# Carrying the recurrence's states over 64-step super-chunks, with an extra 32x32 score block inside each

## The chip, the cores and the metric

The kernel runs on one core of a Trainium2 chip. A core has a matrix engine (TensorE, "PE" in the profile), a vector engine (VectorE, "DVE"), a scalar engine (ScalarE, "ACT"), a general engine (GpSimd, "POOL") and DMA queues. The metric is the device time of one launch in microseconds (us), the median of several runs.

## What is computed

One encoder layer on 512 positions of width 1024, all in float32: a gated feed-forward block, a mixer, a second feed-forward block, a final norm. The mixer adds attention and a two-directional gated recurrence with 8 heads of key and value width 64. The recurrence is what the change touches. The reference computes it in chunks of 32 positions:

```
def gated_scan_chunked(q, k, v, log_f):         # HGRN_CHUNK = 32
    b = jnp.cumsum(log_f, axis=3)                # within a chunk
    b_mid = b[:, :, :, C // 2 - 1:C // 2, :]
    b_last = b[:, :, :, C - 1:, :]
    scores = einsum('bhntd,bhnsd->bhnts', q * exp(b - b_mid), k * exp(b_mid - b))
    o_intra = einsum('bhnts,bhnse->bhnte', where(lower, scores, 0), v)
    contrib = einsum('bhnsd,bhnse->bhnde', k * exp(b_last - b), v)
    # state_n = exp(b_last_n) * state_{n-1} + contrib_n, one after the other over the chunks
    o_inter = einsum('bhntd,bhnde->bhnte', q * exp(b), states_in)
    return o_intra + o_inter
```

The chunk length is a matter of how the sum is grouped: any grouping gives the same outputs up to rounding. The backward direction is the same on the flipped sequence.

## The kernel before

Large products (feed-forward, projections, gates) run as "units": 8 tiles of 128 rows, each tile three passes (`w_hi`x`h_hi`, `w_hi`x`h_lo`, `w_lo`x`h_hi`, lines 952 to 954) of 128x128 weights against 512 moving columns. Every weight block is loaded by DMA into `raw`, split by ScalarE into `w_hi` (line 358) and by VectorE into `w_lo` (line 621, the line of a helper through which all two-operand VectorE steps go).

The recurrence is done in 8 steps u, one for each pair of heads and direction (u // 2 is the pair, u % 2 the direction; two heads lie on partitions 0 to 63 and 64 to 127). Each engine runs its own program in an order written out by hand, tied by semaphores. The steps are woven into the last 16 projection units, the "gate units". On TensorE one round u is: first half of a gate unit (12 matmuls); `contributions(u)` (line 1159: keys times values spread over the chunks of a 128-tile, into two banks of PSUM); second half of the gate unit; `key_transposes(u+1)` (line 1137); `chunk_scores(u+1)` (line 1148); in two rounds a further whole gate unit; `outputs(u)` (line 1175: masked scores times values; line 1180: carried state times query, one matmul for each chunk and head).

The other engines prepare the operands. VectorE: `cumulate` (the running sum `b_cum`, line 823, and `k_sc`, its distance from the middle of a chunk), `mask_scores` (line 854), `query_key` (keys and end-query scaled), `scan_states` (line 865, the states by one scan over 64 value columns x 16 chunks = 1024 elements), gate units' evacuation, and the norm of finished heads. ScalarE: the exponentials (line 508 for `q_sc`, line 513 for `decay`, then `k_sc`, `k_end`, `b_cum`). GpSimd: the query's product (line 291), `k_end` (lines 285 and 295), `k_in` (line 273) and `v_exp` (line 308: values repeated and masked by the four chunks of a tile, 1024 elements for each head). `state` and its two PSUM banks (4 and 5) exist once: `contributions(u)` waits for scan u-1, the scan for `outputs(u-1)`.

In the trace a float32 matmul leaves two records (and two weight loads), so 8 matmuls of `chunk_scores` are 16 records.

## Time and profile before

| what | us |
|---|---|
| median of 3 runs | 1236.41 (1235.05 to 1237.25) |
| profiled execution: span from first to last instruction | 1232.8 |
| TensorE busy in that span | 1201.1 |
| VectorE busy | 639.7 |
| ScalarE busy | 434.3 |
| GpSimd busy | 120.7 |
| mean granted TensorE clock | 0.981 |

The profile page has the busy times, the chain of work that ended last, and groups of instructions. The timeline gives records in order of time with idle time before them; the view of windows gives, for any stretch, the busy time of each engine and the granted TensorE clock (1.00 is 2.4 GHz, 0.50 is 1.2 GHz). A page's span is from first to last instruction; the median of the runs is 3.6 us more than the profiled span.

### The profile page before, as it was taken

To read this page: it belongs to the slowest core of one execution; us is meant where nothing else is said; L and a number is where in the kernel's file an instruction comes from. 1 tells how busy PE (TensorE), PEld (TensorE's weight loads), DVE (VectorE), ACT (ScalarE), POOL (GpSimd) and SP (SyncE) were. 2 spreads that over 40 slices of the span, in tenths; PEclk is the share of its full clock that TensorE was granted. 3 is DMA by queue.
4 is the path that set the end of the run, shared out by engine and by line. 5 is a ranking of instruction groups with operands and counts; after the bars stand their busy time and mean duration, and the time that the engine had idled before them with its cause. 6 is when DMAs were issued, how large, how long until landed. Compare 5 with 4: busy or idle time off the path is not lost.

```text
span 1232.8 us, 16220 instructions
## 1 busy us (share of the span) xinstructions
PE 1201.1 (97%) x6128; PEld 969.9 (79%) x6128; DVE 639.7 (52%) x764; ACT 434.3 (35%) x597; POOL 120.7 (10%) x86
## 2 busy tenths in 40 slices
PE   6999999999999999999999999999999999999995
PEld 5788888888887777777777778888888888888883
DVE  4755555543334844444777754755555555542223
ACT  5333322232223435455754433443322233322210
POOL 3000000000001300000454410012000000000101
PEclk9999999999999999999989999999999999999997
DMA  5332223333214221112211011432223322232201
GB/s 176 119 102 90 91 91 102 121 101 105 98 68 171 69 85 52 69 52 69 69 35 35 22 49 60 166 114 89 93 95 102 102 102 86 94 137 94 94 23 68
DMA packets 28843, 109.83 MB, mean 89 GB/s; under 512 B 3456, under 2 KB 3584, under 8 KB 28416
## 3 DMA queue, kind: packets, MB, share of 16 engines
q1 hardware_dynamic: 26784, 101.72, 24.8%
q10 hardware_dynamic: 2016, 7.50, 1.7%
q8 instruction: 31, 0.51, 0.2%
q14 instruction: 12, 0.10, 0.0%
HBM read 105.02 MB, written 4.19 MB: 89 GB/s over the span
## 4 chain that ended last, share of the span: by engine, by line
PE 95%; DVE 3%; ACT 1%; ACTq 0%; issue 0%; DVEq 0%
PE ps L952 28%; PE ps L954 28%; PE ps L953 28%; PE ps L1180 2%; PE ps L1031 1%; PE ps L1040 1%; PE ps L1056 1%; PE ps L1159 1%; PE ps L1175 1%; DVE xT L621 1%; PE ps L1148 0%; PE ps L981 0%; DVE state L865 0%; PE ps L1091 0%; PE ps L1097 0%
## 5 line engine op out<-in xcount | busy, mean ns | idle before, releaser
L952 PE MATMUL ps<-h_hi,w_hi 128*128 128x512 f32 x1040 | 419.0, 403 | 13.5 <-DVE w_lo L621 9.7
L953 PE MATMUL ps<-h_lo,w_hi 128*128 128x512 f32 x1040 | 410.2, 394 | 0.0
L954 PE MATMUL ps<-h_hi,w_lo 128*128 128x512 f32 x1040 | 410.0, 394 | 0.0
L621 DVE TENSOR_TENSOR w_lo<-raw,w_hi 128x1024 fp32r<-128x1024 f32 (+1 forms) x178 | 234.9, 1320 | 157.1 <-ACT w_hi L358 156.8
L952 PEld LDWEIGHTS ps<-h_hi,w_hi 128*128 128x128 f32 x1040 | 198.3, 191 | 70.9 <-issue 15.7
L358 ACT ACTIVATE w_hi<-raw 128x1024 fp32r<-128x1024 f32 (+1 forms) x178 | 196.8, 1108 | 128.7 <-PE ps L954 125.8
L954 PEld LDWEIGHTS ps<-h_hi,w_lo 128*128 128x128 f32 x1040 | 198.4, 191 | 42.7
L953 PEld LDWEIGHTS ps<-h_lo,w_hi 128*128 128x128 f32 x1040 | 198.7, 191 | 42.3 <-issue 1.9
L952 PE MATMUL ps<-g_hi,w_hi 128*128 128x512 f32 x352 | 136.9, 389 | 0.0
L953 PE MATMUL ps<-g_lo,w_hi 128*128 128x512 f32 x352 | 136.9, 389 | 0.0
L954 PE MATMUL ps<-g_hi,w_lo 128*128 128x512 f32 x352 | 136.9, 389 | 0.0
L386 ACT ACTIVATE g_hi<-un 128x512 f32 (+1 forms) x44 | 27.8, 632 | 249.6 <-DVE un L621 249.6
L621 DVE TENSOR_TENSOR un<-ps,rs 128x512 f32<-128x512 f32 x44 | 30.4, 691 | 119.6 <-PE ps L954 119.6
L952 PEld LDWEIGHTS ps<-g_hi,w_hi 128*128 128x128 f32 x352 | 66.1, 188 | 13.8
L953 PEld LDWEIGHTS ps<-g_lo,w_hi 128*128 128x128 f32 x352 | 66.1, 188 | 13.7
L954 PEld LDWEIGHTS ps<-g_hi,w_lo 128*128 128x128 f32 x352 | 66.1, 188 | 13.7
L366 ACT ACTIVATE sq<-xT 128x512 f32 (+1 forms) x24 | 15.2, 632 | 150.5 <-DVE xT L624 150.5
L624 DVE SCALAR_TENSOR_TENSOR xT<-ps,xT 128x512 f32 (+1 forms) x24 | 16.6, 692 | 95.6 <-PE ps L954 95.6
L244 POOL COPY sq_sum<-sq 128x512 f32<-128x512 f32 x3 | 1.8, 612 | 600.9 <-ACT sq L366 600.9
L621 DVE TENSOR_TENSOR g_lo<-un,g_hi 128x512 f32 (+1 forms) x44 | 30.5, 693 | 39.2 <-ACT g_hi L386 39.2
L247 POOL TENSOR_TENSOR sq_sum<-sq_sum,sq 128x512 f32<-128x512 f32 x20 | 26.0, 1298 | 207.9 <-ACT sq L366 207.9
L624 DVE SCALAR_TENSOR_TENSOR h_lo<-xT,gain,h_hi (+1 forms) x24 | 23.3, 989 | 32.9 <-ACT h_hi L368 25.4
(199 smaller groups left out, 1121.4 us busy)
## 6 DMA issues: line engine op xcount, KB each, us to landing
raw<-up_dram SPq DMA_DIRECT2D x88, 512.0 KB, 3.3
raw<-down_dram SPq DMA_DIRECT2D x32, 704.0 KB, 4.0
raw<-proj_dram SPq DMA_DIRECT2D x26, 512.0 KB, 3.3
raw<-gates_dram SPq DMA_DIRECT2D x16, 512.0 KB, 3.2
raw<-branch_dram SPq DMA_DIRECT2D x8, 512.0 KB, 3.3
raw<-wout_dram SPq DMA_DIRECT2D x8, 512.0 KB, 3.3
xT<-xT_dram ACTq DMA_DIRECT2D x8, 256.0 KB, 6.9
x_spill_dram<-xT ACTq DMA_DIRECT2D x1, 2048.0 KB, 7.4
```

The lines of the kernel that those rows point to most:

```text
L247: nc.gpsimd.tensor_tensor(sq_sum[:], sq_sum[:], sq[:], ALU.add).then_inc(sum_done, 1)
L358: A(w_hi[:, cst % 4, 0:width], raw[:, cst % 2, 0:width], ACT.Copy).then_inc(hi_done, 1)
L366: A(sq[:], xT[:, n, :], ACT.Square).then_inc(sq_done, 1)
L386: A(g_hi[:, 2 * it + q, :], un[:], ACT.Copy).then_inc(ghi_done, 1)
L621: return V.tensor_tensor(out, a, b, op)
L624: return V.scalar_tensor_tensor(out, a, s, b, op0, op1)
L952: T.matmul(ps[:, bank, :], w_hi[:, slot, cols], moving_hi(j), start=start and j == 0, stop=False)
L953: T.matmul(ps[:, bank, :], w_hi[:, slot, cols], moving_lo(j), start=False, stop=False)
L954: ins = T.matmul(ps[:, bank, :], w_lo[:, slot, cols], moving_hi(j), start=False, stop=stop and j == tiles - 1)
L1031: T.matmul(ps[:, 2 + a, :], qk[rows, 1 + t, P * qt:P * (qt + 1)], qk[rows, 0, :], start=True, stop=True).then_inc(s_done, 1)
L1040: ins = T.transpose(ps[:, 4 + a, P * j:P * (j + 1)], prob[:, a, P * j:P * (j + 1)], ident)
L1180: ins = T.matmul(ps[rows, 7, cc], state[rows, :, n + 1 if d else n - 1], b_cum[u % 3][rows, cc], start=False, stop=d == 1 and n == NCH - 2)
```

## The change

States are carried over super-chunks of 64 positions. The running sum restarts every 64 positions, the scan has 8 states for each value column and not 16, `v_exp` has two masks for each 128-tile, not four, and `contributions` fills one bank. Inside a super-chunk the score block between its two 32-chunks is new: `chunk_scores` computes it by 16 more matmuls (8 super-chunks, 2 heads), each 64 rows by 32 weight columns with 32 moving columns, from `kq_far`, the later chunk's queries and the earlier chunk's keys times a factor `fac`. `fac` is a difference of two middles (VectorE, 16 elements) and an exponential (ScalarE, 16 elements); `kq_far` is written half by VectorE, half by GpSimd (256 elements each). `state` and its bank exist twice.

```
-        v_exp = [at("v_exp0", 88, [P, ST, HD, 4]), at("v_exp1", 80, [P, ST, HD, 4])]
-        state = at("state", 84, [P, HD, NCH])
+        v_exp = [at("v_exp0", 88, [P, ST, HD, 2]), at("v_exp1", 80, [P, ST, HD, 2])]
+        kq_far = at("kq_far", 82, [P, NSUP, 2, CHUNK])
+        state = [at("state0", 84, [P, HD, NSUP]), at("state1", 86, [P, HD, NSUP])]
...
             def query(u):                                  # GpSimd
                 nc.gpsimd.tensor_tensor(q_sc[:], q_sc[:], hq[:, u // 2, :], ALU.mult).then_inc(qs_done, 1)
+                pool.wait_ge(qs_done, u + 1)
+                pool.wait_ge(fac_done, u + 1)
+                late = 1 - u % 2
+                nc.gpsimd.tensor_tensor(kq_far[:, :, late, :], supers(q_sc[:])[:, :, CHUNK * late:CHUNK * (late + 1)],
+                                        fac[:, u % 2, :, late].unsqueeze(2).to_broadcast([P, NSUP, CHUNK]), ALU.mult).then_inc(qfar_done, 1)
...
-            pool.wait_ge(spilled, 16)
-            nc.gpsimd.memset(decay[1], 0.0).then_inc(zero_done, 1)
...
                 A(q_sc[:], k_sc[u % 2][:], ACT.Exp).then_inc(e1_done, 1)     # ScalarE
                 if u >= 2:
                     act.wait_ge(state_done, u - 1)
+                act.wait_ge(fd_done, u + 1)
+                A(fac[:, u % 2, :, :], fac[:, u % 2, :, :], ACT.Exp).then_inc(fac_done, 1)
-                n = slice(first, first + NCH - 1)
+                n = slice(first, first + NSUP - 1)
...
             def query_key(u):                              # VectorE
                 tt(k_sc[par][:], k_sc[par][:], k_in[par][:], ALU.mult).then_inc(ks_done, 1)
+                dve.wait_ge(ks_done, u + 1)
+                dve.wait_ge(fac_done, u + 1)
+                tt(kq_far[:, :, par, :], supers(k_sc[par][:])[:, :, CHUNK * par:CHUNK * (par + 1)],
+                   fac[:, par, :, par].unsqueeze(2).to_broadcast([P, NSUP, CHUNK]), ALU.mult).then_inc(kfar_done, 1)
...
             def scan_states(u):                            # VectorE
-                if u:
-                    dve.wait_ge(o_done, u)
+                if u >= 2:
+                    dve.wait_ge(o_done, u - 1)
-                con, flat = ps[:, 4:6, :].rearrange("p a b -> p (a b)"), state[:].rearrange("p e n -> p (e n)")
+                con, flat = ps[:, 4 + u % 2, :], state[u % 2][:].rearrange("p e n -> p (e n)")
...
             def chunk_scores(u):                           # TensorE
+                pe.wait_ge(kfar_done, u + 1)
+                pe.wait_ge(qfar_done, u + 1)
+                early, late = u % 2, 1 - u % 2
+                for n in range(NSUP):
+                    s0 = SUPER * (n % 2) + CHUNK * early
+                    cols = slice(SUPER * n + CHUNK * late, SUPER * n + CHUNK * (late + 1))
+                    for a, rows in enumerate(head_rows):
+                        ins = T.matmul(ps[s0:s0 + CHUNK, 2 + a, cols], kq_far[rows, n, early, :], kq_far[rows, n, late, :],
+                                       start=True, stop=True)
...
             def contributions(u):                          # TensorE
-                if u:
-                    pe.wait_ge(state_done, u)
+                if u >= 2:
+                    pe.wait_ge(state_done, u - 1)
                 for j in range(ST):
-                    for half in range(2):
-                        for a, rows in enumerate(head_rows):
-                            ins = T.matmul(ps[rows, 4 + half, :].rearrange("p (e n) -> p e n", n=NCH)[:, :, 4 * j:4 * j + 4],
+                    for a, rows in enumerate(head_rows):
+                        ins = T.matmul(ps[rows, 4 + u % 2, :].rearrange("p (e n) -> p e n", n=NSUP)[:, :, 2 * j:2 * j + 2],
...
             def outputs(u):                                # TensorE
-                    carried = [n for n in range(4 * j, 4 * j + 4) if n != (NCH - 1 if d else 0)]
+                    carried = [n for n in range(2 * j, 2 * j + 2) if n != (NSUP - 1 if d else 0)]
```

The order on TensorE in round 0, from the end of the gate unit's second half on. Before (`q_sc` and `k_sc` are the scaled queries and keys, `sc_m` the masked scores, `b_cum` by then the end-query):

```order
L1137 MATMUL ps<-small,k_end 128x128 x4
L1148 MATMUL ps<-q_sc,k_sc_76 128x128 x8
L1175 MATMUL ps<-sc_m_82,v_h 64x128 x2
L1180 MATMUL ps<-b_cum_72,state 64x32 x6
L1175 MATMUL ps<-sc_m_82,v_h 64x128 x2
L1180 MATMUL ps<-b_cum_72,state 64x32 x8
```

And at the same place of the changed kernel, where line 1137 is 1156, 1148 is 1167, 1175 is 1202 and 1180 is 1207:

```order
L1156 MATMUL ps<-small,k_end 128x128 x4
L1167 MATMUL ps<-q_sc,k_sc_76 128x128 x8
L1175 MATMUL ps<-kq_far 32x32 x16
L1202 MATMUL ps<-sc_m_84,v_h 64x128 x2
L1207 MATMUL ps<-b_cum_72,state_82 64x64 x2
L1202 MATMUL ps<-sc_m_84,v_h 64x128 x2
L1207 MATMUL ps<-b_cum_72,state_82 64x64 x4
```

Sixteen matmuls have come in behind the scores, and the carried part has half as many, each of twice the columns. On VectorE the same round, before, from the second half of `cumulate(1)` to the state scan:

```order
L621 TENSOR_TENSOR k_sc_76<-b_cum_73 128x512
L854 COPY_PREDICATED sc_m_82<-consts,ps 128x1024
L621 TENSOR_TENSOR k_sc_76<-k_sc_76,sq_sum 128x512
L621 TENSOR_TENSOR b_cum_73<-b_cum_73,hq 128x512
L865 SCALAR_TENSOR_TENSOR state<-decay_84,ps 128x1024
```

And in the changed kernel:

```order
L630 TENSOR_TENSOR k_sc_76<-b_cum_73 128x512
L630 TENSOR_TENSOR fac<-b_cum_73 128x16
L873 COPY_PREDICATED sc_m_84<-consts,ps 128x1024
L630 TENSOR_TENSOR k_sc_76<-k_sc_76,sq_sum 128x512
L630 TENSOR_TENSOR kq_far<-k_sc_76,fac 128x8x32
L630 TENSOR_TENSOR b_cum_73<-b_cum_73,hq 128x512
L884 SCALAR_TENSOR_TENSOR state_82<-decay_86,ps 128x512
```

Two short steps stand ahead of the scan, and the scan covers half the elements.

## Rows read from the trace of the kernel before

**Rows 1.** The page: busy times, and the chain that ended last by line.
```profile
span 1232.8 us, 16220 instructions
PE 1201.1 (97%) x6128; PEld 969.9 (79%) x6128; DVE 639.7 (52%) x764; ACT 434.3 (35%) x597; POOL 120.7 (10%) x86
...
PE 95%; DVE 3%; ACT 1%; ACTq 0%; issue 0%; DVEq 0%
```

**Rows 2.** Groups by line, 560 to 760 us: xcount | busy us, mean ns | idle before.
```profile
L1180 PE MATMUL ps<-b_cum,state 64*64 64x32 f32 x480 | 32.6, 277 | 0.0
...
L308 POOL TENSOR_TENSOR v_exp<-v_h,gain 128x1024 f32<-128x1024 f32 x8 | 18.1, 2288 | 8.3 <-PE ps L1159 8.3
L1159 PE MATMUL ps<-v_exp,sq 128*64 128x128 f32 x256 | 15.7, 276 | 0.0
...
L823 DVE TENSOR_TENSOR_SCAN b_cum<-consts,forget 128x512 f32<-128x512 f32 x8 | 9.7, 1214 | 1.4 <-ACT forget L498 1.4
...
L865 DVE TENSOR_TENSOR_SCAN state<-xT,ps 128x1024 f32<-128x1024 f32 x4 | 9.1, 2286 | 10.5 <-PE ps L1159 10.4
...
L513 ACT ACTIVATE decay<-b_cum 128x960 f32<-128x960 f32 x4 | 7.8, 1950 | 0.0
```

**Rows 3.** Timeline of TensorE, round 2: start us, length us, record, xcount.
```profile
650.26 1.97 PE L1159 MATMUL ps<-v_exp,sq 128*64 128x128 f32 x32
652.16 0.50 PE L952 MATMUL ps<-h_hi,w_hi 128*128 128x512 f32 x1
...
655.55 1.16 PE L1148 MATMUL ps<-q_sc,k_sc 64*128 64x128 f32 x16
656.64 0.44 PE L1175 MATMUL ps<-sc_m,v_h 128*64 128x128 f32 x4
...
658.16 1.07 PE L1180 MATMUL ps<-b_cum,state 64*64 64x32 f32 x16
659.15 0.44 PE L1175 MATMUL ps<-sc_m,v_h 128*64 128x128 f32 x4
```

**Rows 4.** Timeline of TensorE: the records ahead of which it idled.
```profile
607.03 1.16 PE L1148 MATMUL ps<-q_sc,k_sc 64*128 64x128 f32 x16
610.45 0.47 PE L952 MATMUL ps<-h_hi,w_hi 128*128 128x512 f32 x1 [2.26 <-DVE xT L621]
...
621.69 0.44 PE L1175 MATMUL ps<-sc_m,v_h 128*64 128x128 f32 x4 [0.27 <-DVE state L865]
...
672.35 0.44 PE L1175 MATMUL ps<-sc_m,v_h 128*64 128x128 f32 x4 [1.04 <-DVE state L865]
```

**Rows 5.** Windows: stretch, length, busy (x) of PE PEld DVE ACT POOL, PEclk.
```profile
610.45:614.96 4.51, 4.51 (x13) 3.13 (x13) 4.48 (x5) 1.04 (x2) 1.72 (x2) 0.62 0.76 234
...
627.25:632.34 5.09, 5.09 (x14) 3.77 (x12) 2.05 (x2) 3.81 (x6) 2.49 (x3) 0.54 0.00 0
...
656.64:661.89 5.25, 5.25 (x78) 4.40 (x76) 5.15 (x5) 3.71 (x5) 3.42 (x3) 1.00 0.30 100
661.89:664.86 2.97, 2.97 (x15) 2.17 (x13) 2.90 (x3) 0.25 (x1) 2.46 (x2) 1.00 0.00 0
...
677.91:683.16 5.25, 5.25 (x14) 4.13 (x13) 2.04 (x2) 4.60 (x8) 2.49 (x3) 0.50 0.01 3
```

**Rows 6.** Windows: a gate unit's 24 matmuls at full clock and in part throttled.
```profile
705.13:710.80 5.67, 5.67 (x27) 4.43 (x25) 5.59 (x6) 0.57 (x2) 1.17 (x2) 1.00 0.38 113
751.28:758.46 7.18, 7.18 (x26) 5.79 (x25) 1.23 (x1) 2.03 (x3) 0.00 (x0) 0.76 0.24 75
```

**Rows 7.** A small ScalarE step: groups by line and shape, whole span.
```profile
L460 ACT ACTIVATE lbt<-lbt 128x16 f32<-128x16 f32 x1 | 0.2, 204 | 0.0
```

**Rows 8.** Timeline of VectorE ahead of the scan of round 3.
```profile
666.17 0.68 DVE L621 TENSOR_TENSOR k_sc<-k_sc,k_in 128x512 f32<-128x512 f32 x1
...
667.37 2.52 DVE L621 TENSOR_TENSOR yb<-o_u,yb 128x512 fp32r<-128x512 f32 x1
669.92 2.29 DVE L865 TENSOR_TENSOR_SCAN state<-xT,ps 128x1024 f32<-128x1024 f32 x1
```

More of the change, by code:

```diff
@@ L38 @@
 CHUNK = 32
-NCH = S // CHUNK
+SUPER = 2 * CHUNK
+NSUP = S // SUPER
 EPS = 1e-6
@@ L95, in build @@
         norm_v, norm_y, norm_t = (sb(n, [P, ST]) for n in ("norm_v", "norm_y", "norm_t"))
-        gain = sb("gain", [P, 42])
+        gain = sb("gain", [P, 40])
+        fac = sb("fac", [P, 2, NSUP, 2])
         gq8 = sb("gq8", [P, 1])
@@ L253, in _ @@
                     accumulate(n == 0, n, 8 * r + n)
-            nc.gpsimd.memset(decay[0], 0.0).then_inc(zero_done, 1)
+            for d in range(2):
+                nc.gpsimd.memset(decay[d], 0.0).then_inc(zero_done, 1)
             for masked in sc_m:
@@ L262, in _ @@
                 nc.gpsimd.tensor_tensor(q_cos[:, m % 2, :], qk[:, m, :], c["cos"], ALU.mult).then_inc(cos_done, 1)
-            chunks = lambda t: t.rearrange("p (n c) -> p n c", c=CHUNK)
+            supers = lambda t: t.rearrange("p (n c) -> p n c", c=SUPER)
             def key(u):
@@ L282, in to_end @@
                     pool.wait_ge(kt_done, u)
-                b3 = chunks(b_cum[u % 3][:])
-                end = b3[:, :, 0 if u % 2 else CHUNK - 1]
-                nc.gpsimd.tensor_tensor(chunks(k_end[:]), end.unsqueeze(2).to_broadcast([P, NCH, CHUNK]), b3,
+                b3 = supers(b_cum[u % 3][:])
+                end = b3[:, :, 0 if u % 2 else SUPER - 1]
+                nc.gpsimd.tensor_tensor(supers(k_end[:]), end.unsqueeze(2).to_broadcast([P, NSUP, SUPER]), b3,
                                         ALU.subtract).then_inc(d3_done, 1)
@@ L304, in values @@
                     pool.wait_ge(pv_done, ITEMS)
-                shape = [P, ST, HD, 4]
+                shape = [P, ST, HD, 2]
                 for a in range(2):
@@ L308, in values @@
                     nc.gpsimd.tensor_tensor(v_exp[a][:], v_h[:, :, HD * h:HD * (h + 1)].unsqueeze(3).to_broadcast(shape),
-                                            gain[:, 38:42].unsqueeze(1).unsqueeze(1).to_broadcast(shape),
+                                            gain[:, 38:40].unsqueeze(1).unsqueeze(1).to_broadcast(shape),
                                             ALU.mult).then_inc(vexp_done, 1)
-            pool.wait_ge(spilled, 16)
-            nc.gpsimd.memset(decay[1], 0.0).then_inc(zero_done, 1)
             key(0)
@@ L506, in exponentials @@
                     act.wait_ge(sc_done, u)
-                b, first, end = b_cum[u % 3], (1, 0)[u % 2], (CHUNK - 1, 0)[u % 2]
+                b, first, end = b_cum[u % 3], (1, 0)[u % 2], (SUPER - 1, 0)[u % 2]
                 A(q_sc[:], k_sc[u % 2][:], ACT.Exp).then_inc(e1_done, 1)
@@ L826, in cumulate @@
                 mid = b3[:, :, CHUNK // 2 if u % 2 else CHUNK // 2 - 1]
-                tt(chunks(k_sc[u % 2][:]), b3, mid.unsqueeze(2).to_broadcast([P, NCH, CHUNK]), ALU.subtract).then_inc(d1_done, 1)
+                tt(chunks(k_sc[u % 2][:]), b3, mid.unsqueeze(2).to_broadcast([P, 2 * NSUP, CHUNK]), ALU.subtract).then_inc(d1_done, 1)
+                b6 = supers(b[:])
+                if u % 2:
+                    tt(fac[:, 1, :, :], b6[:, :, 16:33:16], b6[:, :, 32:49:16], ALU.subtract).then_inc(fd_done, 1)
+                else:
+                    tt(fac[:, 0, :, :], b6[:, :, 31:48:16], b6[:, :, 15:32:16], ALU.subtract).then_inc(fd_done, 1)
             def normalize(t):
@@ L1147, in chunk_scores @@
                     for a, rows in enumerate(head_rows):
-                        ins = T.matmul(ps[:, 2 + a, cols], k_sc[u % 2][rows, cols], q_sc[rows, cols], start=True, stop=True)
+                        T.matmul(ps[:, 2 + a, cols], k_sc[u % 2][rows, cols], q_sc[rows, cols], start=True, stop=True)
+                pe.wait_ge(kfar_done, u + 1)
[7 more added lines that the diff above has]
+                                       start=True, stop=True)
                 ins.then_inc(sc_done, 1)
@@ L1175, in outputs @@
                         T.matmul(ps[rows, 7, cols], v_h[:, j, HD * h:HD * (h + 1)], sc_m[d][:, a, cols], start=d == 0 and j == 0, stop=False)
-                    carried = [n for n in range(4 * j, 4 * j + 4) if n != (NCH - 1 if d else 0)]
+                    carried = [n for n in range(2 * j, 2 * j + 2) if n != (NSUP - 1 if d else 0)]
                     for n in carried:
-                        cc = slice(CHUNK * n, CHUNK * (n + 1))
+                        cc = slice(SUPER * n, SUPER * (n + 1))
                         for rows in head_rows:
-                            ins = T.matmul(ps[rows, 7, cc], state[rows, :, n + 1 if d else n - 1], b_cum[u % 3][rows, cc],
-                                           start=False, stop=d == 1 and n == NCH - 2)
+                            ins = T.matmul(ps[rows, 7, cc], state[d][rows, :, n + 1 if d else n - 1], b_cum[u % 3][rows, cc],
+                                           start=False, stop=d == 1 and n == NSUP - 2)
                 ins.then_inc(o_done, 1)
@@ L1296 @@
     sin = np.sin(ang).astype(np.float32)[:, p % 32].T * np.where(p % HD < 32, -1.0, 1.0)[:, None]
-    keep = np.broadcast_to(pos[None] % CHUNK != 0, (P, S))
-    same = p[:, None] // CHUNK == p[None] // CHUNK
+    keep = np.broadcast_to(pos[None] % SUPER != 0, (P, S))
+    same = p[:, None] // SUPER == p[None] // SUPER
     mask = np.concatenate([same & (p[:, None] <= p[None]), same & (p[:, None] >= p[None])], axis=1)
```

17 lines of the change are left out of this document (9 added, 8 removed).

## The prediction

> **What bounds the kernel now.** I read the page first. TensorE is busy for 97% of the 1232.8 us span and makes 95% of the chain that ended last [rows 1]. So only what TensorE streams, how fast it is clocked and where it idles can move the time; a faster ScalarE or GpSimd is worth nothing by itself. The groups by line over the recurrence's stretch then give what each kind of small matmul costs in sum [rows 2]; the timeline of one undisturbed round gives the spacing [rows 3]; the idle times ahead of TensorE's records are three, 2.26, 0.27 and 1.04 us, together 3.57 us [rows 4]; and the windows show a fourth quantity, time at the lower clock [rows 5, 6].
>
> **The spacing of small matmuls.** One number carries the sum. In round 2 a run of 16 records of line 1180 (32 moving columns) starts at 658.16 and the next work at 659.15: 62 ns for each record [rows 3]. The 32 records of line 1159, with 128 moving columns each, go from 650.26 to 652.16: 59 ns each. The 16 of line 1148, with 128 weight columns and 128 moving ones, go from 655.55 to 656.64: 68 ns each [rows 3]. So four times the columns costs no more: nothing in these rows lies below 59 ns, and a record of 32 or 64 columns costs some 62.5 ns, whatever is in it. Each matmul is two records.
>
> **What goes on TensorE.** Line 1180 has 480 records, 30 matmuls in each of 8 rounds, as 15 of 16 chunks carry a state. With super-chunks it is 7 of 8, 14 matmuls in a round, 224 records. Their 64 moving columns lie between the 32 and the 128 of rows that both stay near 60 ns, so I take 62.5 again; 256 records fewer are 16.0 us less (the upper price of 68 ns would make it 14.8). Line 1159 has 256 records for 15.7 us [rows 2]; half of them go with the same shape (64 value columns x 2 masks is the 128 that 32 x 4 was): 128 x 59 ns = 7.6 us less.
>
> **What comes.** 16 matmuls in each of 8 rounds are 256 records of 64 rows x 32 weight columns with 32 moving columns. The trace has no such tile. The nearest row is line 1180 with the same 32 moving columns: 62.5 ns, 16.0 us in all. From below: if a smaller tile were quicker, nothing shows by how much; 40 ns, an estimate at two thirds of that row, would give 10.2 us, so a gain of 5.8 more. From above: `outputs(2)` takes 5.25 us [rows 5], of which 60 records of line 1180 are 3.75, so each of its four groups of 4 records of line 1175 takes 0.37, or 92 ns a record with the changes of shape around it; at that price the extra block would be 23.6 us, 7.6 more. I take 62.5 as nearest in shape. A change of tile shape costs too: 4 records of line 1175 at 59 ns would be 0.24 us, they take 0.37, so 0.13 us for a switch. The extra block puts one more switch into each round, 8 x 0.13 = 1.0 us. The work on TensorE then changes by -16.0 - 7.6 + 16.0 + 1.0 = -6.6 us. The Trainium skill (TensorEngine Tiling, "Key Properties") says that changing the tiling mode drains the engine, which speaks against the new block; the trace agrees with a price, 0.13 us as just worked out. It also says (TensorE: Matmul & The Clock Gate, "Wait — 56ns, not 53.3ns?") that small matmuls have a floor of about 25 ns, or about 62 ns where the sequencer decodes them; this trace sits at the latter with 62 ns [rows 3], and by the former the extra block would be an estimated 6.4 us.
>
> **Idle time.** The first idle time, 2.26 us, lies right behind `chunk_scores(0)`, whose records started at 607.03 and ran 1.16 us: TensorE waits until 610.45 for a VectorE evacuation [rows 4]. The 32 new records of that round, 2.0 us, fall into this hole, and GpSimd's `v_exp`, two of 2.29 us each before, is halved [rows 2], so VectorE, which runs slowed beside it, isn't later. The hole closes: 2.26 us back. The other two are waits for the state scan. In round 3 VectorE comes to it late, behind `yb` (2.52 us), and the scan takes 2.29 us [rows 8]. A scan of 512 elements is in the trace at 1.21 us (line 823, [rows 2]), 1.1 us less. Against it stand the new steps on VectorE: 16 elements for `fac`, taken at the 0.2 us that ScalarE needs for as many [rows 7], and 256 elements for its half of `kq_far`, which lie between that and the 0.68 us of 512 elements [rows 8], say 0.4. From one scan's start to the next's end that is -1.1 - 1.1 + 0.2 + 0.4 = -1.6 us, while TensorE gets to its place about 1 us later after the extra block than it would relative to the same scan. Both waits (0.27 and 1.04) go. Idle time: -3.6 us.
>
> **The new waits.** `chunk_scores` now waits also for both halves of `kq_far`. ScalarE's new exponential is 0.20 us [rows 7], but `decay` shrinks from 960 to 448 elements, from 1.95 us to an estimated 0.9 at most, worked out in proportion [rows 2], so everything behind it on ScalarE (`k_sc`, `k_end`, `b_cum`) is about 0.8 us earlier, and VectorE's and GpSimd's products with it. Their additions of 0.4 and some 0.8 us are covered by that and by several microseconds that both have in hand: the keys of step 4 are done at 666.9 [rows 8], and TensorE comes for them at some 670.2, the 16 records of `chunk_scores` ahead of the idle time that ended at 672.35 [rows 4]. Cost 0; were the cover gone in a round, that round would lose at most the 0.8 us. What is queued behind that wait on TensorE is `outputs`, and behind it the next gate unit. Double-buffering frees the scan of `outputs(u-1)`, which no idle time of the trace is due to: 0. The cleared `decay` on GpSimd moves ahead of the recurrence, into its long wait: 0.
>
> **The clock.** The granted clock falls to the lower level six times in this stretch. The first time is behind the idle hole: 610.45 to 614.96 at 0.62, 4.51 us for 12 matmuls that take 2.97 at 1.00 [rows 5]: 1.5 us lost. Four more come at the end of `outputs`, with TensorE busy throughout: 627.25 to 632.34 (5.09, so 2.1 lost) and 677.91 to 683.16 (5.25, so 2.3) are two [rows 5]; a second like the first of these and one of 1.3 us are the others. In three rounds the tail of `outputs` also took 5.56 us, not 5.25, 0.3 more each. The sixth is the unit behind round 7, 7.18 us for the 24 matmuls that otherwise take 5.67 [rows 6]: 1.5 us. Summed: 1.5 + 2.1 + 2.1 + 2.3 + 1.3 + 0.9 + 1.5 = 11.7 us. What ran before five of the six is the same: 5.25 us of `outputs`, 3.8 us of it line 1180, which streams 32 columns in a record's 62 ns. Rounds 2, 4 and 5 had the same and didn't fall ([rows 5], 1.00), so it is near the edge. Lines 1148 and 1159, packed with 128 columns, never precede a fall. In the new kernel `outputs` lasts 4 x 0.37 + 28 x 0.0625 = 3.2 us and its carried records stream twice the columns; only the new block, 2.0 us, is as thin as line 1180 was. I judge that most falls go; I leave one, 2.3 us, so -9.4 us.
>
> **The sum.** -6.6 - 3.6 - 9.4 = -19.6 us, a span of 1213.2, and with the 3.6 us by which the median stands above the profiled span, 1217. Nothing behind the recurrence takes it back: there too TensorE's own lines make the chain [rows 1].
>
> **Rivals.** (a) *The clock goes on falling.* New block and `outputs` stand together, 5.3 us of small tiles against 5.25, and a 64x32 tile fills less of the array than line 1180's 64x64 did. If what keeps the clock up is how much of the array works, and not how many columns stream, the five falls with a busy TensorE stay and only the one behind the hole goes: -6.6 - 3.6 - 1.5 = -11.7, 1225. For it: five falls came with no idle time to explain them. Against it: denser `outputs`. (b) *The extra block is dearer or its waits bite*, at 92 ns a record or with 0.8 us of waiting in each round: 7 us on top of either case, 1224 to 1232. (c) *Slower.* The records of the new tile don't overlap: two heads write one partition range, and each record runs for its own length, 271 ns by line 1180's mean of 277 [rows 2], instead of being followed at 62.5. That is 256 x 0.21 = 54 us, some 1270. It decides from where the spacing passes 0.0625 + 19.6/256 = 0.14 us, with case (a)'s clock from 0.11. Against it: lines 1148 and 1180 alternate the same two row groups and do overlap. (d) *It changes nothing*: the new records cancel the carried ones one for one, 256 against 256, and if the clock falls as often and the block costs 92 ns, 1232 to 1236 is left.
>
> **How the numbers follow.** Forecast, falls mostly gone, 1213 to 1221: 0.52. (a), 1221 to 1229: 0.26. (b) beyond these, up to 1233: 0.10. (c): 0.07. (d): 0.05. A measurement of this kernel can tell about 0.2%, 2.5 us, from no change. Faster by more than that is 0.88, within it 0.05, slower 0.07. The range that holds it 8 times in 10 goes from 1211, all falls gone and a slightly cheaper block, to 1229, the upper end of (a).
>
> **What would show it.** Right: line 1180's successor with 224 records at 62 ns spacing, line 1159's with 128 in half the time; the new block at 2.0 us for 32 records; no idle time behind `chunk_scores(0)` nor ahead of `outputs(0)` and `outputs(3)`; gate halves behind `outputs` at 2.97 us and PEclk 1.00, but for one. Wrong: a spacing in the new block well over 68 ns, waits of TensorE for either half of `kq_far`, or 5 us gate halves at 0.5 behind `outputs`.

## The result and the profile after

The changed kernel takes 1207.74 us (median of 4 runs, 1207.26 to 1207.87), against 1235.73 for the kernel before (4 runs, 1233.88 to 1237.25): a ratio of 0.9781, interval 0.9763 to 0.9799, some 28 us faster. I had forecast 1217 with a range of 1211 to 1229. The direction was right; the time lies below the range.

The page of the changed kernel, the lines that answer to [rows 1]:

```profile
span 1205.5 us, 16026 instructions
PE 1173.3 (97%) x6000; PEld 944.8 (78%) x6000; DVE 636.4 (53%) x780; ACT 428.8 (36%) x605; POOL 119.0 (10%) x94
...
PE 95%; DVE 2%; issue 1%; ACT 0%; ACTq 0%; POOL 0%; DVEq 0%; POOLq 0%
```

The span is 27.3 us shorter. All of it lies between the first `key_transposes` and the last `mean_square`. The view of windows over this stretch (length, busy time of PE, PEld, DVE, ACT and POOL, granted clock), up to where each kernel starts its last `mean_square`, first before (line 1128 starts at 758.46):

```profile
606.50:758.46 151.96, 148.39 (x1295) 118.54 (x1294) 101.98 (x88) 59.90 (x81) 52.08 (x34) 0.90 0.14 46
```

and after, with `outputs(1)` and a gate half behind `outputs(0)`:

```profile
606.91:731.51 124.60, 120.54 (x1167) 92.90 (x1166) 98.49 (x102) 55.22 (x88) 50.93 (x41) 1.00 0.16 54
632.34:636.08 3.74, 3.74 (x54) 2.78 (x45) 3.71 (x4) 1.64 (x3) 2.69 (x2) 1.00 0.46 140
623.51:626.45 2.94, 2.94 (x14) 2.18 (x12) 2.42 (x3) 2.57 (x6) 2.46 (x3) 1.00 0.01 4
```

The stretch went from 151.96 to 124.60 us, 27.4 less, and its clock from 0.90 to 1.00: not one fall is left. `outputs` takes 3.74 us where it took 5.25 [rows 5]. The timeline of TensorE in rounds 1 and 2 (start, length, record, xcount) answers to [rows 3]:

```profile
630.86 1.16 PE L1167 MATMUL ps<-q_sc,k_sc 64*128 64x128 f32 x16
631.95 0.46 PE L1175 MATMUL ps<-kq_far 64*32 64x32 f32 x32
632.34 0.44 PE L1202 MATMUL ps<-sc_m,v_h 128*64 128x128 f32 x4
632.71 0.69 PE L1207 MATMUL ps<-b_cum,state 64*64 64x64 f32 x8
633.33 0.44 PE L1202 MATMUL ps<-sc_m,v_h 128*64 128x128 f32 x4
...
635.69 0.46 PE L1207 MATMUL ps<-b_cum,state 64*64 64x64 f32 x4
636.08 0.50 PE L971 MATMUL ps<-h_hi,w_hi 128*128 128x512 f32 x1
...
639.88 1.09 PE L1186 MATMUL ps<-v_exp,sq 128*64 128x128 f32 x16
640.91 0.50 PE L971 MATMUL ps<-h_hi,w_hi 128*128 128x512 f32 x1
```

The 32 records of the new block, which I had priced at 2.0 us, fill 631.95 to 632.34: 0.39 us. The 16 of `contributions` fill 1.03, not 1.90. Eight carried records with the change of shape ahead of them fill 0.62. The idle times, which answer to [rows 4], are others than before:

```profile
609.63 0.47 PE L971 MATMUL ps<-h_hi,w_hi 128*128 128x512 f32 x1 [0.64 <-DVE xT L630]
617.66 0.66 PE L1156 MATMUL ps<-small,k_end 128*128 128x128 f32 x4 [1.10 <-POOL k_end L304]
659.30 0.44 PE L1202 MATMUL ps<-sc_m,v_h 128*64 128x128 f32 x4 [0.89 <-DVE state L884]
...
667.49 1.13 PE L1147 MATMUL ps<-o_ms,consts 128*128 128x512 f32 x2 [1.43 <-ACT o_ms L555]
```

They sum to 4.06 us, and before to 3.57. From these rows the sum, beside the one forecast (the row on the clock is the time that the kernel before lost in its six falls, as the prediction summed it; none is left):

| term | forecast | measured |
|---|---|---|
| carried matmuls (480 to 224 records) | -16.0 | 8 x (3.74 - 5.25) = -12.1 |
| `contributions` | -7.6 | 8 x (1.03 - 1.90) = -7.0 |
| the extra block, with its change of shape | +17.0 | 8 x 0.39 = +3.1 |
| idle time | -3.6 | 4.06 - 3.57 = +0.5 |
| the lower clock | -9.4 | -11.7 |
| sum | -19.6 | -27.2 |

The error is in one term above all, the block: 13.9 us too dear. The carried matmuls (3.9 us less gained than forecast) and the idle time (4.1 us) err the other way. That the measured median lies only 9.3 us under the forecast is luck of this kind: with the block alone set right, the forecast would have been 1203.

### The profile page after: what moved, and what is told of

It is laid out like the page before. It is cut to its first block, busy times and chain, and to the rows that moved or that the text cites. A ratio compares the mean times of both kernels' runs of the same rounds, so it can differ in the third digit from the quotient of the medians.

```text
span 1205.5 us, 16026 instructions
## 1 busy us (share of the span) xinstructions
PE 1173.3 (97%) x6000; PEld 944.8 (78%) x6000; DVE 636.4 (53%) x780; ACT 428.8 (36%) x605; POOL 119.0 (10%) x94
## 4 chain that ended last, share of the span: by engine, by line
PE 95%; DVE 2%; issue 1%; ACT 0%; ACTq 0%; POOL 0%; DVEq 0%; POOLq 0%
PE ps L971 29%; PE ps L973 28%; PE ps L972 28%; PE ps L1050 1%; PE ps L1075 1%; PE ps L1059 1%; PE ps L1207 1%; PE ps L1202 1%; PE ps L1186 1%; PE ps L1167 0%; PE ps L1000 0%; DVE xT L630 0%; PE ps L1110 0%; PE ps L1116 0%; PE ps L1147 0%
## 5 line engine op out<-in xcount | busy, mean ns | idle before, releaser
L971 PE MATMUL ps<-h_hi,w_hi 128*128 128x512 f32 x1040 | 414.5, 399 | 11.9 <-DVE w_lo L630 9.7
L973 PEld LDWEIGHTS ps<-h_hi,w_lo 128*128 128x128 f32 x1040 | 195.9, 188 | 41.4
L972 PEld LDWEIGHTS ps<-h_lo,w_hi 128*128 128x128 f32 x1040 | 196.1, 189 | 41.0 <-issue 1.9
```

The costliest lines, as they stand in the source:

```text
L971: T.matmul(ps[:, bank, :], w_hi[:, slot, cols], moving_hi(j), start=start and j == 0, stop=False)
L972: T.matmul(ps[:, bank, :], w_hi[:, slot, cols], moving_lo(j), start=False, stop=False)
L973: ins = T.matmul(ps[:, bank, :], w_lo[:, slot, cols], moving_hi(j), start=False, stop=stop and j == tiles - 1)
```

## The experiments

Each is an edit of the changed kernel unless it says otherwise. Times of one run stand without an interval. The theory to be tested was the one the prediction rested on, that any small record costs about 60 ns whatever is in it. The changed kernel's own block refuted it at once; what then sets a spacing had three candidates: (A) the weight load, and with it the stride at which the weights lie, (B) adding into sums that a PSUM bank already holds, (C) how many tiles of the array take turns.

**Without the block.** The matmuls of the extra block are left out, and the mask lets only the 32-step blocks through (not shown in the cut):

```
                 for j in range(ST):
                     for a, rows in enumerate(head_rows):
-                        T.matmul(ps[:, 2 + a, cols], ...)
-                for n in range(NSUP):
-                    ...
-                        ins = T.matmul(ps[s0:s0 + CHUNK, 2 + a, cols], kq_far[rows, n, early, :], kq_far[rows, n, late, :], ...)
+                        ins = T.matmul(ps[:, 2 + a, cols], ...)
```

> The changed kernel without the 256 extra records of the score block on TensorE (kq_far is still computed; the 32x32 blocks between the chunks of a super-chunk are left out, and the mask lets only 32-chunks through). The trace of the changed kernel has the block's 32 records in 0.4 us a round. If that is their whole price: 8 x 0.4 = 3.3 us faster than the changed kernel, some 1204.5. If the block costs what I predicted (16 us + 1 us for the change of tile shape) it would be 1191. If the waits for kq_far cost besides, nothing of that goes, since they stay with the last matmul of the scores only as a semaphore on VectorE's and GpSimd's side; the idle ahead of outputs(3) of 0.9 us should then grow to 1.3.

Measured: 1205.32 us (4 runs, 1205.14 to 1205.68; ratio to before 0.9759, 0.9742 to 0.9775), 2.4 us under the changed kernel, and not 17. Idle time ahead of `outputs(3)` rose from 0.89 to 1.52 us and idle time in all from 4.06 to 5.43, so 1.4 of the 3.1 us came back as waiting; the spans differ by 2.2, 0.5 more than that leaves. The block's price is a few microseconds.

**The block twice.**

```
-                for n in range(NSUP):
+                for n in list(range(NSUP)) * 2:
```

> The changed kernel with every matmul of the extra block issued twice (same outputs). At 12.5 ns a record, as its trace shows: +3.2 us, 1211. At 62.5 ns, the spacing of line 1180: +16 us. If the thin block is what brings the clock down, falls of 2 us a piece appear with it; by the theory of too thin a stretch a doubling to 0.8 us is still short and none appears.

Measured: 1208.65 us (one run), 0.9 more. On TensorE the doubled block of round 1, from the timeline:

```profile
632.18 0.76 PE L1175 MATMUL ps<-kq_far 64*32 64x32 f32 x64
632.86 0.44 PE L1202 MATMUL ps<-sc_m,v_h 128*64 128x128 f32 x4
```

64 records in 0.68 us where 32 took 0.39: a further record costs 9 ns. Eight times 0.29 us is 2.3 us of work, of which idle time gave back 0.8 (3.27 us in place of 4.06). No fall of the clock came with it. The measured whole was even less than the expected 3.2, and the spacing of line 1180 was off by a factor of seven for this tile.

**Carried weights packed**, in the changed kernel and in the kernel before. The weights are 64 adjacent words of the same state tile; both kernels so edited leave out the order in which the states lie, so their outputs are not those of the layer:

```
-                            ins = T.matmul(ps[rows, 7, cc], state[d][rows, :, n + 1 if d else n - 1], b_cum[u % 3][rows, cc],
+                            ins = T.matmul(ps[rows, 7, cc], state[d][:].rearrange('p e n -> p (e n)')[rows, HD * (n + 1 if d else n - 1):HD * ((n + 1 if d else n - 1) + 1)], b_cum[u % 3][rows, cc],
```

> The changed kernel, with the weights of the carried matmuls read as 64 adjacent words of the state tile instead of 64 words 32 bytes apart (they are then the wrong states: the order of the states in the outputs is left out; shapes, counts and accumulation stay). Theory A (the stride of the weights sets the spacing): the 28 records of a round go from 78 ns to 60 or less, 8 x 28 x 0.02 = 4 us or more faster, and their weight loads from 213 ns to the 137 ns of the other 64-column loads. Theory B (adding into a PSUM bank that holds sums sets it): 78 ns stay, same time. Theory C (64 weight columns instead of 32, or two tiles in turn instead of four): 78 ns stay too.

> The kernel before with the same edit (weights of line 1180 adjacent, not 64 bytes apart; the order of the states is left out). Theory A: 480 records at 62.5 ns become 480 at some 20 to 40 ns: 11 to 20 us faster, plus the clock falls that go with the shorter stretch. Theories B and C: 62.5 ns stays and the time is that of before.

Measured: 1204.39 us for the changed kernel so edited (4 runs, 1204.09 to 1204.96; ratio 0.9752, 0.9735 to 0.9768) and 1221.65 (one run) for the kernel before so edited, 13.5 us under its neighbours of 1235.14. The timeline of the latter in round 2, at a clock of 1.00:

```profile
650.87 0.54 PE L1180 MATMUL ps<-b_cum,state 64*64 64x32 f32 x12
651.34 0.44 PE L1175 MATMUL ps<-sc_m,v_h 128*64 128x128 f32 x4
651.71 0.66 PE L1180 MATMUL ps<-b_cum,state 64*64 64x32 f32 x16
652.30 0.44 PE L1175 MATMUL ps<-sc_m,v_h 128*64 128x128 f32 x4
```

and of the kernel before as it is, the run of twelve in the same round (the run of sixteen is in [rows 3]):

```profile
657.01 0.85 PE L1180 MATMUL ps<-b_cum,state 64*64 64x32 f32 x12
657.79 0.44 PE L1175 MATMUL ps<-sc_m,v_h 128*64 128x128 f32 x4
```

The changed kernel with packed weights, in round 0:

```profile
619.98 0.33 PE L1207 MATMUL ps<-b_cum,state 64*64 64x64 f32 x4
620.24 0.44 PE L1202 MATMUL ps<-sc_m,v_h 128*64 128x128 f32 x4
620.61 0.45 PE L1207 MATMUL ps<-b_cum,state 64*64 64x64 f32 x8
620.99 0.44 PE L1202 MATMUL ps<-sc_m,v_h 128*64 128x128 f32 x4
```

And the weight loads of the changed kernel, by line, as it is and packed:

```profile
L1207 PEld LDWEIGHTS ps<-b_cum,state 64*64 64x64 f32 x224 | 16.0, 208 | 5.5 <-issue 5.5
```

```profile
L1207 PEld LDWEIGHTS ps<-b_cum,state 64*64 64x64 f32 x224 | 9.0, 133 | 5.5 <-issue 5.5
```

In the kernel before with packed weights twelve records take 0.47 us and sixteen 0.59, so one more costs 29 ns; as it is, twelve take 0.78 and sixteen 0.99, one more 53 ns. In the changed kernel four records take 0.39 us and eight 0.62, one more 58 ns; packed, four take 0.27 and eight 0.38, 28 ns. Shapes, counts and accumulation were left alone. So A holds and B falls: the stride of the weights doubles the spacing, and 32 or 64 moving columns make almost no difference to it. Theory C isn't touched by this, hence the next two. In the changed kernel the time fell by 3.3 us; of the 7 us less work, 2.8 came back as idle time, which rose to 6.89. In the kernel before, `outputs` went from 5.25 to 3.71 us, 12.3 us less in eight rounds, and idle time rose from 3.57 to 9.03; the rest of its 13.5 us, an estimated 6 to 7, is time at the lower clock that is gone (see below).

**The block on two tiles.**

```
-                for n in range(NSUP):
+                for n in (0, 2, 4, 6, 1, 3, 5, 7):
```

> The changed kernel with the block's matmuls in the order of super-chunks 0 2 4 6 1 3 5 7 (same outputs): now two tiles of the array take turns (one column group, two row groups), where four did. If the number of tiles in turn sets the 12.5 ns, the block's spacing doubles to 20 to 25 ns and a round's block takes 0.7 us, 2 to 3 us in all; if the width of the weights does (32 columns and packed), it stays at 0.4 us and the time at 1207.7.

Measured: 1209.0 us (one run), and by the timeline 32 records from 632.29 to 632.82, 0.53 us in place of 0.39. The spacing went from 12 to 17 ns over the whole block: less than double, but the number of tiles in turn does count. C holds in part. The edit changes nothing but the order; what one more record costs with two tiles wasn't measured apart from the change of shape.

**The block's weights strided.**

```
-        kq_far = at("kq_far", 82, [P, NSUP, 2, CHUNK])
+        kq_far = at("kq_far", 82, [P, CHUNK, NSUP, 2])
...                                                     # the writes of kq_far follow the new layout
-                        ins = T.matmul(..., kq_far[rows, n, early, :], kq_far[rows, n, late, :],
+                        ins = T.matmul(..., kq_far[rows, :, n, early], kq_far[rows, :, n, late],
```

> The changed kernel with kq_far stored so that the block's 32 weight words (and its moving words) lie 64 bytes apart instead of side by side (same outputs). Theory A, the stride: the weight loads take 150 ns or more, not 110, and the block's spacing rises to 25 ns or more, 3 us or more in all. If the stride only matters where sums are added in PSUM, it stays at 12.5 ns. VectorE's and GpSimd's writes of kq_far become strided too, which may cost them some tenths of a us.

Measured: 1210.77 us (one run). The loads by line rose from 108 to 153 ns, and the 32 records of a round fill 0.66 us (633.18 to 633.84) in place of 0.39, 20 ns each:

```profile
L1176 PEld LDWEIGHTS ps<-kq_far 64*32 64x32 f32 x256 | 4.8, 153 | 1.0
```

That is A for the new block too, in a place where nothing is added up across matmuls. The edit puts the 32 moving words at a stride as well; the longer loads are the weights' own, but how much of the 20 ns the moving side adds isn't separated. The spacing came out at 20, a little under the expected 25. VectorE's writes of `kq_far` went from 1.12 to 1.49 us, as expected, a cost of the same edit.

**Carried part twice**, and **carried part in halves.** These two tell what went with the falls of the clock. The first issues each carried matmul twice (so the carried part counts double in its outputs), the second issues it as two of 32 columns; the `stop` flags follow and are not shown:

```
-                    for n in carried:
+                    for i, n in enumerate(carried * 2):
```

```
                     for n in carried:
-                        cc = slice(SUPER * n, SUPER * (n + 1))
+                      for part in range(2):
+                        cc = slice(SUPER * n + CHUNK * part, SUPER * n + CHUNK * (part + 1))
```

> The changed kernel with every carried matmul issued twice (the carried part is added twice, so it counts double in the outputs): 448 records of 64 moving columns at 78 ns instead of 224, outputs of 5.9 us instead of 3.74, longer than the 5.25 of the kernel before but with twice the columns in each record. Work alone: +17.5 us, 1225. If the length of the stretch of small tiles brings the clock down, falls come back in most rounds, 2 us each, 1233 to 1240. If the columns per time do (64 columns in 78 ns against 32 in 62), no falls, 1225.

> The changed kernel with each carried matmul of 64 moving columns issued as two of 32 (same outputs): 448 records, as many in a round as in the run with the carried part twice, but each as thin as line 1180 of the kernel before. Outputs of about 5.0 us. If what lowers the clock is how few columns stream per time, falls come back in several rounds, 2 us each: 1219 + 4 to 12 us. If it was the idle time and the length alone, none come, as none came with the carried part twice (5.2 us of outputs, 1219.8): 1219 or a little less.

Measured: 1219.78 us and 1232.06 us, one run each, 12.3 apart for the same 448 records. The windows of `outputs(1)` and the gate half behind it, carried part twice:

```profile
634.60:640.02 5.42, 5.42 (x82) 4.46 (x73) 4.87 (x6) 3.31 (x6) 4.67 (x5) 1.00 0.23 82
640.02:642.87 2.85, 2.85 (x14) 2.36 (x13) 0.89 (x2) 2.73 (x4) 1.46 (x2) 1.00 0.03 6
```

and in halves:

```profile
634.07:639.39 5.32, 5.32 (x82) 4.47 (x73) 4.76 (x6) 3.31 (x6) 4.59 (x4) 1.00 0.21 82
639.39:643.83 4.44, 4.44 (x15) 3.50 (x14) 0.98 (x2) 2.73 (x4) 1.54 (x2) 0.62 0.02 4
```

Both `outputs` are longer than the 5.25 us of the kernel before; TensorE is busy throughout in both; idle time in the stretch is the same, 1.75 and 1.76 us. With 64 columns in each record no clock fall comes in any round. With 32 the clock falls behind `outputs` in seven of eight rounds, here for 1.6 us (4.44 against 2.85), and its mean over the span is 0.980, not 0.993. So neither length nor idle time did it, but how few columns stream in the stretch.

The kernel before with packed weights shows that it isn't the 32 columns of a record either, but how closely such records follow. It has the same 480 records of 32 columns in the same 64x64 tiles, at 29 ns in place of 53. `outputs(0)`, the gate half behind it, and `outputs(3)`:

```profile
621.55:625.26 3.71, 3.71 (x77) 2.86 (x77) 3.67 (x5) 0.25 (x1) 0.92 (x1) 1.00 0.42 126
625.26:628.19 2.93, 2.93 (x15) 2.17 (x12) 1.12 (x2) 2.93 (x4) 1.88 (x2) 1.00 0.07 25
667.30:673.57 6.27, 6.27 (x77) 4.69 (x77) 4.68 (x5) 2.81 (x3) 2.79 (x2) 0.50 0.26 84
```

Of the six falls two are left, and each lies behind idle time: the hole of 2.24 us in round 0 and a wait of 3.71 us for the scan ahead of `outputs(3)`. None comes behind an `outputs` that TensorE reached without a wait, where the kernel before had three in that way, in rounds 1, 6 and 7. That was the mechanism of the forecast. Rival (a) falls in the form it had: the tiles are 64x64 in all these kernels, so the area of the array alone doesn't decide. Whether area counts beside the columns is not tested.

**The waits of before.** The states stay double, but the scan and `contributions` wait as in the kernel before (`if u: ... wait_ge(o_done, u)` and `wait_ge(state_done, u)`).

> The changed kernel with the waits of a single state: the scan u waits for outputs(u-1), contributions(u) for scan u-1. I predicted double-buffering at 0: the same time within 1 us. If it matters, some 1 to 3 us slower.

Measured: 1207.52 us (4 runs, 1207.46 to 1208.13; ratio 0.978, 0.9755 to 0.9804), the same as the changed kernel. The looser waits that double-buffering allows are worth nothing here.

**The new steps on VectorE.** In the changed kernel the 16-element `fac` takes 1.02 us on VectorE. The timeline shows what it runs beside, first VectorE, then GpSimd:

```profile
612.38 0.69 DVE L630 TENSOR_TENSOR k_sc<-b_cum 128x512 f32<-128x512 f32 x1
612.99 1.02 DVE L630 TENSOR_TENSOR fac<-b_cum 128x16 f32<-128x16 f32 x1
613.93 1.36 DVE L873 COPY_PREDICATED sc_m<-consts,ps 128x1024 f32<-128x1024 uint32 x1
```

```profile
612.42 1.55 POOL L289 TENSOR_TENSOR k_end<-b_cum 128x512 f32<-128x512 f32 x1 [5.23 <-DVE b_cum L833]
613.93 1.30 POOL L295 TENSOR_TENSOR q_sc<-q_sc,hq 128x512 f32<-128x512 f32 x1
```

It ends when GpSimd's `k_end` does, in all eight rounds, where VectorE's steps of 4 elements take 0.16 us. No run has it beside an idle GpSimd, so that GpSimd's step is the cause is an inference; VectorE's half of `kq_far` supports it, with 0.42 us in the two of eight rounds in which GpSimd stood still and 1.15 to 1.41 beside a step of GpSimd. Three steps follow from there, each on top of the one before it. First `fac` moves to GpSimd, ahead of `k_end`:

```
             def to_end(u):                               # GpSimd
+                if u >= 2:
+                    pool.wait_ge(kfar_done, u - 1)
...
+                nc.gpsimd.tensor_tensor(fac[:, u % 2, :, :], b3[:, :, lo], b3[:, :, hi], ALU.subtract).then_inc(fd_done, 1)
```

> The changed kernel with the 16-element difference for fac on GpSimd, ahead of its k_end, not on VectorE (same outputs). On VectorE it took 1.02 us, begun while GpSimd's 512-element k_end ran. If it is the meeting of the two that makes 16 elements cost 1.02 us, VectorE is 1.0 us a round earlier, the idle time ahead of outputs(3) (0.9) goes and that ahead of mean_square (1.4) shrinks, 1 to 2 us faster, 1206. If VectorE's lateness isn't what these waits hang on, the same time.

Measured: 1206.94 us (4 runs, 1206.79 to 1207.06; ratio 0.9773, 0.9756 to 0.9789), 0.8 us less. On GpSimd it takes 0.73 us, and the waits ahead of `outputs(3)` and `mean_square` fell from 0.89 and 1.43 us to 0.62 and 0.94, but those ahead of round 0's gate half and of its `k_end` grew from 0.64 and 1.10 to 1.16 and 1.38. Idle time in all is 4.10 us against 4.06, and the profiled spans differ by 0.2 us: the step is dear on either engine, and moving it only shifts the waits.

Then ScalarE reads the finished outputs ahead of three exponentials:

```
             def exponentials(u):                         # ScalarE, behind the decay exponential
+                if u >= 3 and u % 2:
+                    outputs_to_sbuf(u // 2 - 1)
```

> The same, and ScalarE reads finished outputs out of PSUM behind the decay exponential of the round, ahead of the three exponentials that stood before it (same outputs). TensorE's 1.4 us wait for o_ms in round 4 should go: 1 to 1.5 us faster than without. Against it: the three exponentials come up to 1.2 us later, which the keys of the next round could miss.

Measured: 1206.32 us (4 runs, 1205.23 to 1207.15; ratio 0.9765, 0.9749 to 0.9781). The wait for `o_ms` is gone, and two timings gained the 1.5 us; the two others show a mean clock of 0.991, not 0.994, and the profiled one of these has a fall behind `outputs(3)`, whose start it waited 0.61 us for. The median is 0.6 us lower, not the expected 1 to 1.5.

Then ScalarE copies the states so that the 64 values of a super-chunk lie side by side:

```
+                A(state_n[u % 2], state[u % 2][:].rearrange("p e n -> p n e"), ACT.Copy).then_inc(packed_done, 1)
...
-                            ins = T.matmul(ps[rows, 7, cc], state[d][rows, :, n + 1 if d else n - 1], ...)
+                            ins = T.matmul(ps[rows, 7, cc], state_n[d][rows, n + 1 if d else n - 1, :], ...)
```

> The same, and ScalarE copies the states (512 elements, 0.63 us) so that a super-chunk's 64 values lie side by side for the weight load (same outputs). From the run with packed weights: 28 records a round at 47 ns and not 78, 7 us less work. The copy lengthens the way from the scan to outputs by 0.7 us, which costs idle time where the scan is late (round 3, perhaps 0 and 2): 1 to 3 us back. Some 4 us faster than without it, 1200 to 1202.

Measured: 1206.01 us (4 runs, 1201.11 to 1206.16; ratio 0.9766, 0.9749 to 0.9782): one timing at 1201.11 with a clock of 0.994, three at 1205.91 to 1206.16 with 0.989 or 0.990. The profiled run is the quick one; it waits 2.62 us for the packed states ahead of `outputs(3)` and has no fall there. The expected 1200 to 1202 came in one timing of four, and the median is hardly under the 1206.32 of the kernel without the copy. Where the other three lost their clock no trace shows.

**Packed or not, with the scan ahead.** In both kernels VectorE runs the scan of rounds 1, 3 and 5 ahead of the end-query's product and of `yb_lo`:

```
-            def query_key(u):
+            def query_key(u, then=None):                 # VectorE
...                                                       # behind kq_far
+                if then is not None:
+                    scan_states(then)
                 dve.wait_ge(e4_done, u + 1)
```

> The kernel with packed states, and in rounds 1, 3 and 5 VectorE runs the scan ahead of the end-query's product and of yb_lo (same outputs). The 2.62 us wait for the packed states in round 3 should shrink by the 1.4 us of these two steps. If the three slower timings of the packed kernel (1206 against 1201, at a clock of 0.990 against 0.994) come from a fall of the clock behind that wait, all timings should now be at 1200 or less. If they come from outputs being thin (64 columns in 47 ns are not), the spread stays.

> The same order of the scan with strided states (same outputs as the kernel with early outputs). Its wait of 0.61 us for the scan goes, and with it the fall of the clock seen in round 3 of that kernel (clock 0.991 in two of four timings): 1205 or a little less in all timings. The difference between the two kernels of this pair is the packing alone: by the spacings, 7 us of work less 1.5 us of added waits.

Measured: packed 1202.11 us (4 runs, 1201.44 to 1202.38; ratio 0.9733, 0.9717 to 0.9749), strided 1205.37 (4 runs, 1204.94 to 1205.71; ratio 0.9759, 0.9743 to 0.9775), all eight at a clock of 0.994. In the packed one:

```profile
658.51 0.44 PE L1215 MATMUL ps<-sc_m,v_h 128*64 128x128 f32 x4 [1.29 <-ACT xT L590]
658.88 0.45 PE L1220 MATMUL ps<-b_cum,xT 64*64 64x64 f32 x8
659.26 0.44 PE L1215 MATMUL ps<-sc_m,v_h 128*64 128x128 f32 x4
```

The 2.62 us wait is down to 1.29 and the spread is gone. The packing alone is worth 3.3 us: idle time is 5.63 us against 2.55, so 3.1 us of the expected 7 are waiting, where 1.5 were expected. The packed kernel is the quickest of all, 5.6 us under the changed kernel. It did not reach the 1200 or less that I had expected.

## Why the prediction was wrong, step by step

**The bound.** Right: TensorE makes 95% of the chain before and after, and the whole difference is found in what it streams, its idle time and its clock.

**The spacing of small matmuls, the step that failed.** The prediction says "nothing in these rows lies below 59 ns, and a record of 32 or 64 columns costs some 62.5 ns, whatever is in it", and prices the new block at that: 16.0 us, and 1.0 for the change of shape. The rows that I read were three shapes that came near 60 ns, not for one reason. Line 1180 did so for weights at a stride: with packed weights the same records follow at 29 ns, so nothing that a record costs by itself holds it at 62. Line 1159 has packed weights; its 128 moving columns are the likely reason, which no run here tests. A floor can't be read off rows when none of them is small in every dimension. The runs showed in its place: one more record with 64 packed weight columns costs 28 or 29 ns and with strided ones 53 to 58, at 32 as at 64 moving columns; one more with 32 packed weight columns and four tiles in turn costs 9. The trace of before held a hint that I averaged away: runs of 12 and of 16 records of line 1180 differ by 53 ns a record, so 0.14 us of each is the change of shape and not spacing. The Trainium skill (TensorE: Matmul & The Clock Gate, "LDWEIGHTS (loading the stationary operand)") puts a weight load at its columns over 1.2 GHz, whatever its rows: 53 ns for 64 columns. Shared by two tiles in turn that would be an estimated 27 ns a record, and the packed runs agree, 28 and 29; that a stride doubles it is only in the runs.

**The extra block.** Forecast 16.0 us and 1.0 for the change of shape, measured 3.1. My range for it began at an estimated 40 ns a record, 10.2 us; the measured 12 ns lies far below, and with it the time fell out of the range. The Trainium skill's floor of some 25 ns for a small matmul (the same page, "Wait — 56ns, not 53.3ns?"), which I had cited and by which the block would have been an estimated 6.4 us, would have been nearer; with several tiles in turn the rows go below that too. That two heads writing one partition range might not overlap, rival (c), is refuted by the same rows.

**Carried matmuls.** Forecast -16.0, measured -12.1. Half of the records went, but the changes of shape stayed, four into the carried part in each round at 0.14 us, and 64-byte stride became 32-byte stride at about the same cost, 58 ns against 53.

**Contributions.** Forecast -7.6, measured -7.0, the mechanism and size right.

**Idle time.** Forecast -3.6, measured +0.5. The hole behind `chunk_scores(0)` shrank from 2.26 to 0.64 us and did not close: VectorE's evacuation releases TensorE 1.2 us sooner behind the start of the scores (2.19 us in place of 3.42), but the block fills 0.39 us of the gap and not 2.0. The waits for the scan of rounds 0 and 3 were to go; that of round 0 did, round 3 has 0.89. Two others came, for GpSimd's `k_end` (1.10) and for ScalarE's `o_ms` (1.43). The failed step is the cover of "several microseconds", which I had read in one round. In round 1 of the kernel before GpSimd ends `k_end` less than a microsecond before TensorE comes for it; first the two rows of before, then `k_end` of after, for which TensorE waits until 617.66:

```profile
617.50 1.30 POOL L295 TENSOR_TENSOR k_end<-k_end,sq_sum 128x512 f32<-128x512 f32 x1 [1.46 <-ACT k_end L518]
619.74 0.60 PE L1137 MATMUL ps<-small,k_end 128*128 128x128 f32 x4
```

```profile
616.32 1.28 POOL L304 TENSOR_TENSOR k_end<-k_end,sq_sum 128x512 f32<-128x512 f32 x1 [0.39 <-ACT k_end L527]
```

`k_end` is done 1.2 us sooner, at 617.60, and TensorE is there 3.2 us sooner, at 616.56: its clock no longer falls behind the hole and `contributions` takes half the time. So a gain on TensorE came back in part as a wait. The prices of the new steps were wrong too: `fac` on VectorE at 0.2 us took 1.02, and `kq_far` there at 0.4 took that only beside an idle GpSimd and 1.12 on average. But they don't make the waits by themselves: with `fac` off VectorE idle time stayed at 4.10 us. GpSimd's new product, which I had named, didn't delay `k_end` here, as GpSimd stood idle for 0.39 us behind it.

**Double-buffering.** Forecast 0; taking its looser waits back changed nothing, 1207.52 against 1207.74 us.

**The clock.** Forecast -9.4 with one fall left, measured -11.7 with none. The mechanism was right: the pair of runs with equal records and unequal columns shows it, and the kernel before with packed weights agrees. That the area of the array alone keeps the clock up is refuted. One later kernel had a fall behind a wait of 0.61 us ahead of `outputs(3)`, and the kernel with packed states showed a mean clock of 0.989 or 0.990 in three timings of four; both are at 0.994 in all timings since the scan was moved ahead. It isn't settled how much idle time it takes: the changed kernel waits 0.89 us there and the profiled run with packed states 2.62, neither with a fall, and the kernel before with packed weights fell behind 3.71.

## What to carry to other kernels

Price a small matmul of this kind by its weight load before its columns: how many weight columns, whether they lie side by side, and how many tiles of the array take turns. A layout that is handy for the engine that writes a tile, here the scan, can double the price on the engine that reads it as weights, and a copy on an idle engine may pay, here 3.3 us once the wait that it brought was shortened. Don't read a floor off rows that merely agree; look for two runs of different length of the same shape and take the difference. When TensorE gets quicker ahead of a wait, look in each round at how much earlier its operands are done than it comes for them. And where TensorE's clock falls although it is busy, look at the stretch ahead for matmuls with few moving columns that follow each other slowly.

## What the runs showed of the hardware that was not expected

- Weights at a stride: 208 ns for a load of 64 columns at 32 bytes against 133 packed, and 53 (64 bytes) to 58 ns (32 bytes) from record to record against 29 and 28, with two tiles in turn. For 32 columns at 64 bytes 153 against 108 ns, and 20 ns against 12 over four tiles.
- 32 float32 records of 64x32 weights and 32 moving columns, over four tiles of the array, take 0.39 us with the change of shape, and 32 more only 0.29.
- The clock falls with TensorE busy all the time: 448 records of 32 columns brought it down in seven of eight rounds, 448 of 64 columns in none, for 12.3 us between two kernels with the same number of records. 480 records of 32 columns at 29 ns in place of 53 brought it down in no round except behind idle time.
- The stride costs nothing at the lower clock: sixteen packed records of line 1180 fill 1.00 us at 0.50 (`outputs(3)` of the kernel before with packed weights, 667.92 to 668.92), sixteen strided ones of the kernel before 1.02 us at 0.50 (626.23 to 627.25) and 0.99 at 1.00.
- A subtraction of 16 elements took 1.02 us on VectorE beside a step of GpSimd, and ended with it; on GpSimd it took 0.73. A product of 256 elements took 0.42 us with GpSimd idle and about 1.4 beside its `k_end`.
